# Gated linear attention: state products of 64 columns accumulated into halves of a tile's region, and one decayed q without zeros

## The reference, cut to what matters

```python
def gla_chunked(q, k, v, log_a):
    C = GLA_CHUNK            # 64
    qc, kc, vc, gc = to_chunks(q), to_chunks(k), to_chunks(v), to_chunks(log_a)
    b = jnp.cumsum(gc, axis=-2)
    ...
    o_intra = jnp.einsum('nbhij,nbhjv->nbhiv', A, vc)
    q_inter = qc * jnp.exp(b)
    ...
    def step(state, inp):
        qi, ki, vi, di = inp
        o = jnp.einsum('bhid,bhdv->bhiv', qi, state)
        state = state * di[..., None] + jnp.einsum('bhjd,bhjv->bhdv', ki, vi)
        return state, o
```

## Time and profile before

| | us |
|---|---|
| median of 3 runs (lowest, highest) | 2650.29 (2650.02, 2654.04) |
| the profiled execution, its own time | 2646.91 |
| its span in the profile | 2645.1 |
| PE busy | 2354.6 |
| DVE busy | 1288.0 |
| ACT busy | 1023.8 |
| POOL busy | 455.2 |

### The profile page before, as it was taken

How to read it: one execution, slowest core, us unless ns; L and a number is a source line. 1 busy time by engine, 2 the same in 40 slices (tenths; PEclk the granted TensorE clock), 3 DMA queues, 4 the chain that set the end, 5 groups by cost and what they waited for, 6 DMA issues and landing times. The chain is left out here.

```text
span 2645.1 us, 31291 instructions
## 1 busy us (share of the span) xinstructions
PE 2354.6 (89%) x11004; PEld 1767.1 (67%) x11004; DVE 1288.0 (49%) x2049; ACT 1023.8 (39%) x1655; POOL 455.2 (17%) x494
## 2 busy tenths in 40 slices
PE   7999677898999994988799998998988899998997
PEld 4877355764444443767687886886767687886885
DVE  4278677324111116446516775344446616775344
ACT  5221366222111114556453444234556453444233
POOL 1058143111222213211220000002211221000000
PEclk9999798899999995999999998998999999999998
DMA  6200300124999986101110003012101110003012
GB/s 195 84 32 1 127 1 1 10 96 149 348 347 331 303 267 257 41 25 32 32 42 21 11 33 128 32 65 82 40 25 33 32 42 21 11 33 128 32 56 80
DMA packets 207787, 239.69 MB, mean 91 GB/s; under 512 B 45088, under 2 KB 165152, under 8 KB 207648
## 3 DMA queue, kind: packets, MB, share of 16 engines
q1 hardware_dynamic: 197680, 221.06, 25.2%
q0 software_dynamic: 8928, 16.80, 1.7%
q10 hardware_dynamic: 1040, 0.00, 0.0%
HBM read 212.13 MB, written 41.42 MB: 96 GB/s over the span
## 5 line engine op out<-in xcount | busy, mean ns | idle before, releaser
L106 PE MATMUL ps<-WT_lo,HT_hi 128*128 128x512 f32 x832 | 326.3, 392 | 0.0
L107 PE MATMUL ps<-HT_hi,WF_lo 128*128 128x512 f32 x800 | 316.6, 396 | 0.0
L105 PE MATMUL ps<-HT_hi,WU_hi 128*128 128x512 f32 x704 | 288.7, 410 | 16.2 <-DVE H_lo L2173 12.2
L106 PE MATMUL ps<-H_lo,WU_hi 128*128 128x512 f32 x704 | 279.0, 396 | 0.0
L1594 PE MATMUL ps<-WT,MIX 128*128 128x512 f32 x496 | 225.8, 599 | 4.8 <-DVE MIX L2132 4.8
L105 PE MATMUL ps<-W_hi,HT_hi 128*128 128x512 f32 x512 | 204.2, 399 | 8.8 <-DVE MIX_lo L2316 5.9
L948 POOL TENSOR_TENSOR WF_lo<-WF,WU_hi 128x1024 fp32r<-128x1024 f32 x44 | 113.8, 2586 | 539.9 <-ACT WU_hi L1175 539.9
L107 PE MATMUL ps<-W_hi,MIX_lo 128*128 128x512 f32 x512 | 201.4, 393 | 0.0
L106 PEld LDWEIGHTS ps<-WT_lo,HT_hi 128*128 128x128 f32 x832 | 158.2, 190 | 31.5
L107 PEld LDWEIGHTS ps<-HT_hi,WF_lo 128*128 128x128 f32 x800 | 153.5, 192 | 33.2
L105 PEld LDWEIGHTS ps<-HT_hi,WU_hi 128*128 128x128 f32 x704 | 136.0, 193 | 51.1 <-DVE H_lo L2173 13.0
(11 more groups left out here) (432 smaller groups left out, 5051.7 us busy)
## 6 DMA issues: line engine op xcount, KB each, us to landing
WT<-in_w_gate SPq DMA_DIRECT2D x31, 1024.0 KB, 5.8
WT<-in_w_up SPq DMA_DIRECT2D x31, 1024.0 KB, 9.4
MIX<-in_w_down SPq DMA_DIRECT2D x31, 1024.0 KB, 8.8
WF<-in_w_in SPq DMA_DIRECT2D x48, 512.0 KB, 3.9
WT<-in_w_out SPq DMA_DIRECT2D x6, 2048.0 KB, 8.1
H<-in_x SPq DMA_DIRECT2D x16, 512.0 KB, 8.2
h_dram<-H SPq DMA_DIRECT2D x16, 512.0 KB, 3.0
H<-h_dram SPq DMA_DIRECT2D x16, 512.0 KB, 10.7
```

The source lines that it names most:

```text
L105: pe.matmul(o, lh, rh, start=(i == 0), stop=False)
L106: pe.matmul(o, lh, rl, start=False, stop=False)
L107: mm = pe.matmul(o, ll, rh, start=False, stop=(i == last))
```

## The change

In each tile the two state products cover 64 columns each, the columns of their own chunk, and accumulate into the halves of the region that the first product has written. The decayed q is then stored once (`q_dec`), by one DVE operation over 1024 columns in place of two strided ones of 512. POOL's memset of the zeros (L951) goes, and `z_ready` is raised by the memset of `wgs` instead.

```diff
-        q_even, q_odd = slot(WTf, 2), slot(WTf, 3)
+        q_dec = slot(WTf, 2)
...
                 unit_lo(0)
-                pool.memset(wgs, 0.0)
-                pool.memset(WT[:, 0, 4:KD, :], 0.0).then_inc(z_ready, 1)
+                pool.memset(wgs, 0.0).then_inc(z_ready, 1)
                 pool.memset(lr_rows[0:32, :].bitcast(F32), 0.0).then_inc(lz_ready, 1)
                 unit_lo(1)
...
                     for t in range(NT):
                         ts = slice(t * P, (t + 1) * P)
-                        mm = accumulate(pe, bank(6 + t // 4, P, (t % 4) * P), [(gv[h % 2][:, ts], Asum[:, ts]),
-                                                                             (st[:, 2 * t, :], q_even[:, ts]), (st[:, 2 * t + 1, :], q_odd[:, ts])])
+                        b, at = 6 + t // 4, (t % 4) * P
+                        pe.matmul(bank(b, P, at), gv[h % 2][:, ts], Asum[:, ts], start=True, stop=False)
+                        for c in range(2):
+                            mm = pe.matmul(bank(b, CH, at + CH * c), st[:, 2 * t + c, :], q_dec[:, t * P + CH * c:t * P + CH * (c + 1)], start=False, stop=(c == 1))
                     mm.then_inc(g_pe, 1)
...
                     if h >= 1:
                         dve.wait_ge(*gla(L, "o", h - 1))
-                    for par, to in ((0, q_even), (1, q_odd)):
-                        v = lambda a: a.rearrange("p (t c i) -> p t c i", t=NT, c=2)[:, :, par, :]
-                        o = dve.tensor_tensor(v(to), v(cum), v(q), ALU.mult)
-                    o.then_inc(g_dve, 1)
+                    dve.tensor_tensor(q_dec, cum, q, ALU.mult).then_inc(g_dve, 1)
```

## The result

The changed kernel is slower: median 2659.41 us against 2650.12 us (12 runs each), ratio 1.0034, 95% interval 1.0024 to 1.0044. That is 9.3 us, above the 0.2% that the prediction called measurable. On another chip the ratio was 1.0038 (1.0025 to 1.0051). The forecast was 2652.2 us, "the same", with a range up to 2655.5.

What follows compares the result with a forecast made beforehand. TensorE, busy 89% of the span, was taken as the bound. Products 0, q -0.3 and POOL's turn in layer 1 +2.2 gave +1.9 us on the 2650.29 us median: 2652.2 us, range 2647.5 to 2655.5 us.

Steps and rivals of the forecast that it cites:

- Products, heads 0 to 2, at 0: TensorE's state products there keep 0.112 us a record at 64 columns, since weight loading sets the pace: 0 us.
- Rival E: Columns, not weights, set a record's pace; a full-clock tile takes 0.45 us, total 2648.8 us; chance 5%.
- Products of head 3, "I take 0", bounds 0 to -2.3 us: TensorE's products after the 6.25 us wait: narrow records gain nothing at the low clock; at most 2.3 us saved.
- rival C: Narrow records are quick even at the low clock, as weight loads don't slow with it: 2649.9 us; chance 10%.
- Rival F: Narrow products drop the clock to 1.2 GHz in all eight product stretches: +15.3 us, 2667.5 us; chance 4%.
- the 62-column stretch of the earlier trace: 32 TensorE records with full weights and 62 moving columns at clock 1.00: 0.112 us each, taken as evidence for unchanged pace.
- q at -0.3 us: DVE's decayed q as one 1.22 us operation instead of 1.29 us, counted on the path four times: -0.3 us.
- POOL's memset, loads, `lr_rows` and `products` at nothing: Removing the 1.80 us memset starts gate-weight loads and lr_rows's memset earlier and frees DVE's products' semaphore: worth nothing.
- L948 earlier, +2.2 us in layer 1, none in layer 0: At layer start, POOL's earlier L948 blocks DVE's fourth H_lo subtraction in layer 1 only, delaying TensorE: +2.2 us.
- the fourth is running; L948 waits: Layer 0's start: L948 at 1049.7 finds DVE's fourth H_lo subtraction running, waits until 1050.6: no change for TensorE.
- Rival D: L948 blocks DVE in both layers, needing layer 0's L948 0.25 us earlier than worked out: 2654.4 us; chance 6%.
- The forecast of 8.2 us for this wait: TensorE's wait for H_lo at layer 1's start grows from 6.1 to 8.2 us, L948 beginning during the third subtraction.

Runs made afterwards that it cites:

- before_head3_narrow: Kernel before with 64-column state products in head 3 alone, the rest unchanged: 2657.15 against 2648.18 us, ratio 1.0030.
- after_filled: after_memset_back plus 24 unread 512-column matmuls on TensorE in the wait for head 3's states: 2644.06 us against 2648.17 us for the kernel before, 0.9982.
- before_memset_late: Kernel before with POOL's memset of WT moved behind the second unit's L948, nothing else changed: 2653.22 against 2648.18 us, 1.0019.
- after_pool_waits: Changed kernel with POOL waiting for DVE's fourth H_lo subtraction before L948: 2655.42 us against 2649.66 us for the kernel before, 1.0021.
- after_memset_back: Changed kernel with POOL's memset of WT put back in its old place: 2654.49 us against 2648.18 us for the kernel before, 1.0022.
- before_moved: Kernel before with head 3's products moved behind the next unit's first half, its squares behind the second: 2633.94 against 2648.17 us, 0.9943.
- after_head3_wide: Changed kernel with head 3's state products over 128 columns again (output differs): 2652.74 us against 2648.18 us for the kernel before, 1.0015.

## Why the prediction was wrong, point by point

- *Products, heads 0 to 2, at 0:* right. The pace is 0.112 us a record at 64 columns, nothing lost by adding into halves, and the waits for the squares stayed. Rival E is refuted by the rows at 1151 us.
- *Products of head 3, "I take 0", bounds 0 to -2.3 us:* this step failed, its bounds included. Its reading of a record was right: at the low clock a narrow tile takes as long as a wide one (1335.24 - 1324.97 = 10.3 us for eight, 1.28 each), and rival C is refuted. What it left out is that the number of tiles run at the low clock is not given. It took the 3.9 and 5.2 us at 0.50 of the kernel before as fixed. But there the clock rose within the wide products; within the narrow ones it didn't rise at all: it returned only in the next unit, after 14.3 and 12.6 us. The term measured +5.1 and +3.6 us in the profiled pair, and before_head3_narrow puts it at +9.0 us of the median by itself. What it is about the narrow products that leaves the clock low is not shown; TensorE counted as busy throughout.
- *Rival F, the clock drops in the products, 4%:* the nearest to the truth, and still with the wrong place and sum. For head 3 alone it had the price of the products almost right (+2.9 and +2.3 us, measured +3.1 and +2.4), though not that of the half unit behind them (+2.0 and +1.2). But it looked for a drop in all eight stretches and took the 62-column stretch of the earlier trace rows as evidence against it. That stretch began at full clock, so it could show only that narrow records keep a clock that is there, which the stretches at 1150.90 and, in after_filled, 1324.50 confirm. For head 3, where the clock was already low, it said nothing.
- *q at -0.3 us:* one operation of 1.22 us, as forecast, in six of eight heads (3.38 in head 0 of each layer, where an L948 starts 0.7 us or less before it); too small to be measured alone.
- *POOL's memset, loads, `lr_rows` and `products` at nothing:* nothing in the profile after speaks against it.
- *L948 earlier, +2.2 us in layer 1, none in layer 0:* the mechanism was right, the place too narrow. It struck both layers, +2.5 us each, and before_memset_late measures it at +5.0 us. The step that failed was layer 0's "the fourth is running; L948 waits". In the kernel after the fourth subtraction and L948 stand like this in the timeline:

```profile
1050.20 3.72 DVE L2174 TENSOR_TENSOR H_lo<-MIX,HT_hi 128x1024 fp32r<-128x1024 f32 x1
1050.51 2.33 POOL L948 TENSOR_TENSOR WF_lo<-WF,WU_hi 128x1024 fp32r<-128x1024 f32 x1
```

  DVE's record starts 0.31 us ahead, and still POOL runs through unhindered while DVE ends 1.08 us after it. The prediction had worked out this same distance (1049.40 and 1049.7) and read it as DVE's turn. Rival D, 6%, had this outcome, but not by its reason: L948 came no earlier than worked out.

  Layer 1 was hit, but not as forecast (the fourth subtraction, L948 beginning during the third). POOL and DVE there, first the first subtraction, then the third:

```profile
1845.21 2.35 POOL L948 TENSOR_TENSOR WF_lo<-WF,WU_hi 128x1024 fp32r<-128x1024 f32 x1 [5.45 <-ACT WU_hi L1174]
1845.27 3.37 DVE L2174 TENSOR_TENSOR H_lo<-MIX,HT_hi 128x1024 fp32r<-128x1024 f32 x1 [2.34 <-issue]
...
1848.99 2.98 POOL L948 TENSOR_TENSOR WF_lo<-WF,WU_hi 128x1024 fp32r<-128x1024 f32 x1
1849.70 3.36 DVE L2174 TENSOR_TENSOR H_lo<-MIX,HT_hi 128x1024 fp32r<-128x1024 f32 x1
```

  In the kernel before, POOL's first L948 started 0.28 us behind DVE's first subtraction (1838.60 and 1838.32) and had to wait for it; here it starts 0.06 us ahead, so that the hits fall one earlier. The forecast of 8.2 us for this wait (8.7 measured) came near over another sequence.

  The Trainium skill, "SBUF — State Buffer", section "Who interferes with whom", says that a DVE instruction with two SBUF inputs contends with a GpSimd instruction that reads SBUF and not with one that only writes. The traces agree: L948 blocks DVE for 2.2 to 2.5 us, the memset at 1048.81 of the earlier trace rows doesn't. Its statement that issue order decides who blocks agrees with the starts in layer 1, where 0.06 us was enough and DVE came out of idleness. It doesn't help with 1050.20 and 1050.51, where DVE's record starts first and POOL has the turn: that record starts before the third subtraction has ended (1046.90 + 3.38 = 1050.28), so its start isn't the moment at which the turn is decided. When that moment is, the runs don't show.
- *Sum:* the terms forecast were 0 for head 3 and +2.2 for POOL. With +5.0 for POOL and +6 to +9 for head 3 (after_pool_waits, after_memset_back, before_head3_narrow), the two measured parts pass the 9.3 us found; by 1.0019 and 1.0030 one would expect 1.0049, by 1.0019 and 1.0022 (after_memset_back) 1.0041, against 1.0034 and 1.0038 measured. Each interval is 0.2 to 0.25% wide, so the difference is not resolved.

## What to carry to other kernels

Where every matmul loads new weights of 128 columns, halving its moving columns to 64 gained nothing here (0.67 us a tile at full clock, 1.28 at the low one), and behind a wait it cost 6 to 9 us over the two layers. So count which stretches start at the low clock, and don't take the length of the low clock from a kernel that moved more columns in them. When removing an instruction that nobody waits for, look at what moves up behind it and which operation it blocks; on POOL that was a DVE operation on the critical path, +2.5 us in each layer. The better lever here was the 6.25 us wait itself: half a unit moved into it gave 14 to 15 us in before_moved, mostly as wait (6.25 to 0.86 us in each layer), the rest as clock.

## What the runs showed that was not expected

- 24 useless matmuls of 512 columns in a wait made the kernel 10.6 us faster than without them, with the 48 products behind them at 5.4 us instead of 10.3 and the next unit started at full clock.
- The low clock lasted 14.3 us through uninterrupted work of TensorE, of which 10.3 us were products with 64 and 128 columns; with 128 columns alone it ended after 4.1 and 3.6 us (after_head3_wide, layers 0 and 1). TensorE was idle in neither: the profile counts 14.23 of 14.30 us and 4.03 of 4.10 us as busy. A weight load takes 333 ns there and 192 ns at full clock, with 64 columns as with 128:

```profile
L1704 PEld LDWEIGHTS ps<-WT x32: 333/333/333, 1325.4 to 1335.0; 128*128 128x128 f32 x32
...
L1704 PEld LDWEIGHTS ps<-WT x32: 192/192/192, 1151.2 to 1156.2; 128*128 128x128 f32 x32
```
